# A stack of three transformer layers: raw weight buffers cut from four to two

## The reference

```python
# first and second layer, with sandwich norms
h = rms_norm(x, g[0])
m = parallel_conv_mla(h, ...) if first else conformer_conv(h, ...)
x = x + rms_norm(m, g[1])
h = rms_norm(x, g[2])
x = x + rms_norm(relu(h @ w1) ** 2 @ w2, g[3])          # 1024 -> 4096 -> 1024
# parallel_conv_mla: h @ w_in; a 3-tap gated convolution on one half; on the other
#   q = rms_norm(q_lat) @ w_uq, k and v = rms_norm(kv_lat) @ w_ukv, rotary parts of q and k,
#   8 heads of softmax attention; both halves joined @ w_out
# conformer_conv: u = a * sigmoid(g); 31-tap depthwise convolution; layer norm; silu; @ w_pw2
# third layer: 16 meta tokens put ahead
#   q, k, v, forget gates, u = rmsnorm(h) @ w_in; causal attention with the prefix sums of
#   log forget gates added to the logits; four trailing means of u through w_pool; @ w_out
#   h + (silu(n2 @ w_gate) * (n2 @ w_up)) @ w_down        # 1024 -> 2816 -> 1024
```

## Time and profile before

| | before |
|---|---|
| median of 3 runs | 2021.57 us (2020.75 to 2026.03) |
| the profiled execution | 2022.05 us |
| its span in the profile | 2020.3 us |
| mean granted clock of TensorE | 0.954 of full |
| busy: PE / DVE / ACT / POOL | 1925.0 / 1065.7 / 562.2 / 927.8 us |
| weight loads | 286, 512.0 KB each |
| read from HBM over the span | 77 GB/s |

### The profile page before, as it was taken

The page is one execution under the profiler, slowest core; times in us unless marked ns, Lnnn a source line. Parts: engine busy times, 40 slices in busy tenths (PEclk is TensorE's granted clock), DMA queues, the critical chain, the costliest instruction groups (busy, mean ns, idle before and its releaser), DMA issues.

```text
span 2020.3 us, 23937 instructions
## 1 busy us (share of the span) xinstructions
PE 1925.0 (95%) x8603; PEld 1571.6 (78%) x8603; DVE 1065.7 (53%) x1318; ACT 562.2 (28%) x822; POOL 927.8 (46%) x478
## 2 busy tenths in 40 slices
PE   7898999999999989899999999999999999999999
PEld 5776877878888767687878888788777778888887
DVE  4886667811863598676830674546233234444300
ACT  4225623111121343343112112232232133222221
POOL 7355445434444479835434444432211154444443
PEclk9999999999999999999999999999955599999999
DMA  4152022323233122211323233221100023332332
GB/s 170 49 146 63 1 84 63 96 91 93 94 98 100 52 63 84 83 54 56 101 84 102 94 94 99 67 63 64 57 7 1 0 84 94 101 96 93 104 104 73
DMA packets 46677, 157.80 MB, mean 78 GB/s; under 512 B 6545, under 2 KB 6801, under 8 KB 46609
## 3 DMA queue, kind: packets, MB, share of 16 engines
q1 hardware_dynamic: 46608, 156.86, 24.8%
HBM read 152.58 MB, written 2.10 MB: 77 GB/s over the span
## 4 chain that ended last, share of the span: by engine, by line
PE 72%; DVE 18%; POOL 5%; issue 3%; ACT 1%; DMA 0%; DVEq 0%; SPq 0%; POOLq 0%; ACTq 0%
PE PS L1435 23%; PE PS L1436 22%; PE PS L1437 22%; DVE tmp L915 3%; DVE HL L907 2%; POOL acc_p L499 2%; DVE HH L1169 2%; DVE XL L915 2%; POOL wl L488 2%; DVE tmp L907 1%; DVE X L907 1%; PE PS L1445 1%; DVE ssq L907 1%; PE PS L1594 1%; DVE sqb L907 1%
## 5 line engine op out<-in xcount | busy, mean ns | idle before, releaser
L431 POOL TENSOR_TENSOR wl<-raw,wh 128x1024 fp32r<-128x1024 f32 x244 | 602.4, 2471 | 790.0 <-ACT wh L582 484.2
L1435 PE MATMUL PS<-XH,wh 128*128 128x512 f32 x1440 | 575.6, 400 | 41.5 <-DVE XL L915 25.2
L1437 PE MATMUL PS<-XH,wl 128*128 128x512 f32 x1440 | 565.5, 393 | 0.0
L1436 PE MATMUL PS<-XL,wh 128*128 128x512 f32 x1440 | 565.5, 393 | 0.0
L1435 PEld LDWEIGHTS PS<-XH,wh 128*128 128x128 f32 x1440 | 273.6, 190 | 113.0 <-issue 36.0
L582 ACT ACTIVATE wh<-raw 128x1024 fp32r<-128x1024 f32 x152 | 161.1, 1061 | 668.2 <-PE PS L1437 668.2
L1437 PEld LDWEIGHTS PS<-XH,wl 128*128 128x128 f32 x1440 | 273.3, 190 | 58.4
L1436 PEld LDWEIGHTS PS<-XL,wh 128*128 128x128 f32 x1440 | 273.8, 190 | 53.5
L1435 PE MATMUL PS<-HH,wh 128*128 128x512 f32 x688 | 269.6, 392 | 8.4 <-DVE HL L907 8.4
L1436 PE MATMUL PS<-HL,wh 128*128 128x512 f32 x688 | 269.2, 391 | 0.0
L1437 PE MATMUL PS<-HH,wl 128*128 128x512 f32 x688 | 268.9, 391 | 0.0
(11 more groups left out here) (265 smaller groups left out, 2479.5 us busy)
## 6 DMA issues: line engine op xcount, KB each, us to landing
raw<-weights SPq DMA_DIRECT2D x286, 512.0 KB, 3.5
X<-x_t SPq DMA_DIRECT2D x8, 256.0 KB, 8.2
out_t<-X SPq DMA_DIRECT2D x8, 256.0 KB, 4.6
KH<-rope_h SPq DMA_DIRECT2D x4, 128.0 KB, 4.5
KL<-rope_l SPq DMA_DIRECT2D x4, 128.0 KB, 5.4
QH<-XH SPq DMA_DIRECT2D x16, 32.0 KB, 2.0
QL<-XL SPq DMA_DIRECT2D x16, 32.0 KB, 2.0
pos_i<-positions SPq DMA_DIRECT2D x1, 256.0 KB, 9.3
```

Of the source, the lines that this page charges most:

```text
L431: pool.tensor_tensor(wl[:, j], raw[:, j], wh[:, j].bitcast(F32), ALU.subtract).then_inc(w_lo, 1)
L1435: pe.matmul(out, wa, xa, start=start, stop=False)
L1436: pe.matmul(out, wa, xb, start=False, stop=False)
L1437: return pe.matmul(out, wb, xa, start=False, stop=stop)
```

## The change

`raw` shrinks from four buffers to two (`RAW = 2`); `wh` and `wl` keep four. Block n is loaded into buffer n % 2 once low part n - 2 is made, and the counts that ScalarE waits for on `raw_in` are those of two semaphores that each serve every second block. At the start blocks 0 and 1 are loaded among the X tiles as before, and blocks 2 and 3 come in `load_range` behind X7, positions and meta tokens. The boundaries of the load ranges around the second and third group of side transfers move by two blocks, from 28 to 26 and from 206 to 204; the one around the first stays at 16.

```diff
+RAW = 2
-        raw = sb("raw", [P, RING, SLOTS, P])
+        raw = sb("raw", [P, RAW, SLOTS, P])
-        raw_in = [sem(f"raw_in{j}") for j in range(RING)]
+        raw_in = [sem(f"raw_in{j}") for j in range(RAW)]
...
             for k in range(KT):
                 sp.dma_start(X[:, k], x_t[:, k]).then_inc(x_in[k], 16)
-                if k in (0, 2):
-                    sp.dma_start(raw[:, k // 2 + 1], weights[k // 2 + 1]).then_inc(raw_in[k // 2 + 1], 16)
-            sp.dma_start(raw[:, 3], weights[3]).then_inc(raw_in[3], 16)
+                if k == 0:
+                    sp.dma_start(raw[:, 1], weights[1]).then_inc(raw_in[1], 16)
...
             def load(n):
-                sp.wait_ge(w_lo, n - RING + 1)
-                sp.dma_start(raw[:, n % RING], weights[n]).then_inc(raw_in[n % RING], 16)
+                sp.wait_ge(w_lo, n - RAW + 1)
+                sp.dma_start(raw[:, n % RAW], weights[n]).then_inc(raw_in[n % RAW], 16)
...
-            load_range(RING, 16)
+            load_range(RAW, 16)
...
-            load_range(16, BLOCK0["w_out"] + 4)
+            load_range(16, BLOCK0["w_out"] + RAW)
...
-            load_range(BLOCK0["w_out"] + 4, BLOCK0["w_in_2"] + 14)
+            load_range(BLOCK0["w_out"] + RAW, BLOCK0["w_in_2"] + 12)
...
-            load_range(BLOCK0["w_in_2"] + 14, NBLK)
+            load_range(BLOCK0["w_in_2"] + 12, NBLK)
...
                 j = n % RING
-                sc.wait_ge(raw_in[j], 16 * (n // RING + 1))
+                sc.wait_ge(raw_in[n % RAW], 16 * (n // RAW + 1))
                 if n >= RING:
                     sc.wait_ge(blocks_done, n - RING + 1)
-                sc.activation(wh[:, j], raw[:, j], ACT.Copy).then_inc(w_hi, 1)
+                sc.activation(wh[:, j], raw[:, n % RAW], ACT.Copy).then_inc(w_hi, 1)
```

More of the change, by code:

```diff
@@ L358, in load_range @@
                     for j in range(RING):
-                        sp.wait_ge(w_lo, g * RING + (j - RING + 1))
-                        sp.dma_start(raw[:, j], weights[g * RING + j]).then_inc(raw_in[j], 16)
+                        sp.wait_ge(w_lo, g * RING + (j - RAW + 1))
+                        sp.dma_start(raw[:, j % RAW], weights[g * RING + j]).then_inc(raw_in[j % RAW], 16)
                 for n in range(b // RING * RING, b):
                     load(n)
-            load_range(RING, 16)
+            load_range(RAW, 16)
             sp.wait_ge(rope_done, 1)
@@ L421, in lo @@
                     pool.wait_ge(w_hi, n + 1)
-                    pool.tensor_tensor(wl[:, n % RING], raw[:, n % RING], wh[:, n % RING].bitcast(F32),
+                    pool.tensor_tensor(wl[:, n % RING], raw[:, n % RAW], wh[:, n % RING].bitcast(F32),
                                        ALU.subtract).then_inc(w_lo, 1)
@@ L430, in lo_range @@
                             pool.wait_ge(w_hi, g * RING + (j + 1))
-                            pool.tensor_tensor(wl[:, j], raw[:, j], wh[:, j].bitcast(F32), ALU.subtract).then_inc(w_lo, 1)
+                            pool.tensor_tensor(wl[:, j], raw[:, j % RAW], wh[:, j].bitcast(F32), ALU.subtract).then_inc(w_lo, 1)
                 for n in range(max(a, b // RING * RING), b):
@@ L464, in _ @@
                 pool.wait_ge(w_hi, n + 1)
-                pool.tensor_tensor(wl[:, n], raw[:, n], wh[:, n].bitcast(F32), ALU.subtract).then_inc(w_lo, 1)
+                pool.tensor_tensor(wl[:, n], raw[:, n % RAW], wh[:, n].bitcast(F32), ALU.subtract).then_inc(w_lo, 1)
             add_squares("x0")
@@ L487, in lo_to @@
                     pool.wait_ge(w_hi, i + 1)
-                    pool.tensor_tensor(wl[:, i % RING], raw[:, i % RING], wh[:, i % RING].bitcast(F32),
+                    pool.tensor_tensor(wl[:, i % RING], raw[:, i % RAW], wh[:, i % RING].bitcast(F32),
                                        ALU.subtract).then_inc(w_lo, 1)
@@ L579, in hi_range @@
                         for j in range(RING):
-                            sc.wait_ge(raw_in[j], g * 16 + 16)
+                            sc.wait_ge(raw_in[j % RAW], g * (16 * RING // RAW) + 16 * (j // RAW + 1))
                             sc.wait_ge(blocks_done, g * RING + (j - RING + 1))
-                            sc.activation(wh[:, j], raw[:, j], ACT.Copy).then_inc(w_hi, 1)
+                            sc.activation(wh[:, j], raw[:, j % RAW], ACT.Copy).then_inc(w_hi, 1)
                     a += rounds * RING
@@ L883, in _ @@
                     slot = (n0 + j) % RING
-                    sc.wait_ge(raw_in[slot], g * 16 + 16 * ((n0 + 4 + j) // RING + 1))
+                    sc.wait_ge(raw_in[slot % RAW], g * (16 * RING // RAW) + 16 * ((n0 + 4 + j) // RAW + 1))
                     sc.wait_ge(blocks_done, n - RING + 1)
-                    sc.activation(wh[:, slot], raw[:, slot], ACT.Copy).then_inc(w_hi, 1)
+                    sc.activation(wh[:, slot], raw[:, slot % RAW], ACT.Copy).then_inc(w_hi, 1)
                     if j % 2:
```

## The result

The changed kernel takes 2058.4 us (median of 4 runs, 2050.6 to 2060.7) against 2023.4 (4 runs), a ratio of 1.0166 with a 95% interval of 1.0134 to 1.0198: 34 us slower, where 23 were predicted. The direction and the five places hold; the time lies above the range. Its profiled execution was its quickest, 2050.57 us (span 2048.8), 28.5 above the one of before, so the sum of what that one trace shows is 5 to 8 us short of the medians.

What follows compares the result with a forecast made beforehand. TensorE was taken to bound the kernel (72% of the chain, VectorE 18%), with loads hidden. Five serial terms, 4.1 + 10.7 + 1.35 + 1.35 + 5.8 = 23.3 us, gave 2044.9 us, range 2034 to 2055.

Steps and rivals of the forecast that it cites:

- Steady stretch: MLPs, output projections and FFN: loads still land ahead of use, with slack 3.7 us instead of 14.6; 0 us.
- convolution phase: GpSimd's low parts there do not wait, with 1.6 us to spare in the tightest pattern; 0 us, at most 6.5.
- Start: Raw block 2 waits behind X3 to X7, positions and meta, delaying TensorE's work after it: +4.1 us, ends 0 and 5.2.
- K rope transfers: After load 15: two loads come an estimated 5 us later, hidden by low parts made 12.8 us ahead; 0 us.
- Q rope transfers: Loads 26 and 27 stand behind 32 DMAs, delaying V copies and first-layer attention: +10.7 us, ends 10.5 and 16.9.
- Entries of phases: Block n0+7 lands late in the opening burst: +1.35 us each at pw1 and w_in_2, 0 at the other entries.
- Decay transfers: Loads n0+12 and n0+13 of w_in_2 stand behind 32 small DMAs, delaying the last pool product: +5.8 us, ends 5.3 and 8.4.
- Hidden transfers: Rival: two buffers suffice also at SyncE's side transfers, only the start costs: 2025.7 us, chance 4%.
- waiting blocks: Rival: landings later than 7.2 us make every block wait: 2160 us with one us over, chance 2%.
- the rope term: Delay of first-layer attention at Q's rope transfers, +10.7 us; the rival that only this fails: 2034.2 us, chance 9%.
- fast clock: Rival: third layer's attention gets more time at full clock; no slower from 41 us, about 2013 with 50; chance 4%.
- slow clock: Rival: first layer's attention starts at half clock after 14 us of idling: some 20 us more, 2065, chance 8%.

Runs made afterwards that it cites:

- o3: Kernel before, four raw buffers, with only loads 2 and 3 put behind the X tiles, positions and meta: 2028.3 us, ratio 1.0020.
- o1: Kernel before, four raw buffers, with only loads 26 and 27 put behind the 32 rope transfers of Q: 2036.3 us, ratio 1.0055.
- f4: Changed kernel, loads 26 and 27 among Q's rope transfers, w_in_2 load 12 before decay transfers, fourth high parts at pw1 and w_in_2 entries moved later: 2030.9 us.
- f3: Changed kernel with the fourth high part at the entries of pw1 and w_in_2 moved later on ScalarE: 2051.9 us, ratio 1.0135.
- o2: Kernel before, four raw buffers, with only loads 12 and 13 of w_in_2 put behind the 32 decay transfers: 2033.5 us, ratio 1.0044.
- f2: Changed kernel with the load of block 12 of w_in_2 put ahead of the decay transfers: 2049.8 us, ratio 1.0114.
- g3: Changed kernel with GpSimd's low parts 12 and later of w_in_2 held until VectorE has made the pool operands' low parts: 2051.6 us, ratio 1.0150.
- h4: The changed kernel itself measured again, unaltered: 2060.1 us, ratio 1.0168.
- h1: Changed kernel with rope, decay and entries mended, and GpSimd's low parts 7 and 10 in w_in held until VectorE's sums: 2024.9 us, ratio 1.0006.

## Why the prediction was wrong, by its steps

- *Steady stretch, convolution phase: 0 us.* Right; from 1640 us on there is no wait for a raw block, and in the convolution phase none delayed GpSimd or TensorE.
- *Start, +4.1.* Right: 4.0 (o3, 1.8 to 6.3). Block 2 was 3.4 late.
- *K rope transfers, 0.* No shift shows there.
- *Q rope transfers, +10.7.* Right: 11.1 (o1, 8.5 to 13.8), with 3.81 from issue to use where 3.5 was taken.
- *Entries of phases.* "At the first entry ... nothing urgent stands behind `hi(n0+7)`: 0" failed: on ScalarE nothing did, but GpSimd's low part behind it fell beside VectorE's sum, with half clock behind TensorE's wait for it: 2.7 us (f4 against o3), 2.5 in f4's trace. pw1, +1.35: 1.2 in the trace. w_in_2, +1.35: the stall is right at 1.36, the term failed, as it took the clock behind the stall as unchanged. f3's 6.5 less 1.2 leave 5.3.
- *Decay transfers, +5.8, at most 8.4.* Failed: 8.9 (o2), 10.7 less when mended (f2). The stall by itself is the forecast (5.5 in g3); the term took VectorE's two low parts at their usual 0.69 us each, and beside GpSimd they make it 8.0 (9.6 in h4). Behind it 2.2 more gather by the matmul at 1424 us of before, most of it at half clock; the third layer takes back 1.9.
- *Sum.* 4.0 + 11.1 + 8.9 from the orders, 6.5 from two entries, 2.7 in w_in: 33.2 of 33.8. Missing in the forecast were 3.9 at w_in_2, 3.1 at decay and 2.7 in w_in, 9.7 of the 10.5 us that part 33.8 from 23.3. That it comes out so closely is in part luck: each of these numbers is known to 2 to 5 us. The other 3 us of the miss (2058.4 against 2044.9) are no term: before's median is 2023.4 over four runs, not the 2021.6 over three that I started from, and the changed kernel's median lies a little over its ratio.
- *Rivals.* Hidden transfers and waiting blocks didn't come, and the rope term held. Of the fast clock came 1.9 us, in the third layer. The slow clock did not cost where I had put it: behind the 12.8 us of idling the clock was halved until 195 us, and the warming matmuls spent that time (7.03 us for 22, 6.91 before); the scores ran at 1.00. It came as short stretches behind the new waits in w_in, in w_in_2 and at the pool block. The range had each landing's bounds and none for what a stall does to the clock.

The misses have one root: I followed a late block along semaphores only. The two other paths need no semaphore. That VectorE waits for GpSimd shows in the rows: f4's sum, begun 0.06 us after the low part of 2.40 us, takes 2.88 us where 0.69 is usual, and ends 0.54 us after it. The Trainium skill, "SBUF — State Buffer", states in its section "Who interferes with whom" that a VectorE instruction with two SBUF inputs contends with a GpSimd instruction that reads SBUF, and in its summary of rules that the second of them to issue is blocked until the first finishes. The rows agree, and with the low parts held (g3, h1) the same operations take 0.69 us, and 1.29 for two.

## What to carry to other kernels

Shrinking a ring costs where the queue has other work ahead of a load: test it by giving the larger ring the smaller one's order, since here that alone was 24 of 34 us. With the rope, decay and entry places mended, two buffers came within 7 us of four (f4), and with low parts held in both within 3.4, about what the start costs. When a wait is predicted, price three things: the wait, the clock of TensorE behind it, and which VectorE operation the late GpSimd operation now falls beside. A stall of 1.4 us was followed by a loss of 0, 1.7, 5 or 10 us in different profiles. And a gain or loss of a few us may be the clock of another stretch: compare the shift at several points, not only the time.

## What the hardware showed unexpectedly

- Idling for 1.1 to 1.5 us was followed by TensorE at 1.2 GHz for 3.4, 10 or 20.5 us of busy time in seven of eight profiles, and by 2.4 GHz in one. With the gap filled by 7 matmuls it stayed at 2.4 GHz in the one profile taken.
- In the third layer the same matmuls spent 130 to 143 us at 1.2 GHz, depending on edits far ahead of them, and the time moved by up to 7 us with it.
- VectorE's 128x512 operation with two operands took 0.69 us alone and up to 2.9 beside a 2.4 us low part of GpSimd; two in a row took 5.11, and 1.29 with GpSimd held back.
